# Turning half of the router's input inside the output projection of a two-layer transformer kernel

## The chip, the cores and the metric

The kernel runs on one core of one Trainium2 chip. The metric is device time in microseconds (us) of one execution; lower is better. The kernel before was timed in three runs: 1039.24, 1039.88 and 1039.9 us, median 1039.88 us.

## The reference, cut to what matters

All arithmetic is float32 on 256 tokens of width 1024. A first block (dilated attention, latent attention, a dense feed-forward) is followed by a second block of two layers. Each layer of the second block ends in the same four steps, and these are what the change touches:

```
h = h + mix @ w_out                                   # output projection, 1024 x 1024
xn = rms_norm(h, ln_ffn[i])
g_prob = softmax(xn @ w_group + b_group)              # 4 groups
e_logits = xn @ w_expert + b_expert                   # 32 experts, the best 2 of the best group
h = h + sum over the chosen experts (silu(xn @ w_gate) * (xn @ w_up)) @ w_down
gate = sigmoid(rms_norm(h, ln_ple[i]) @ ple_w_gate[i])
h = h + gate * (p[i] @ ple_w_proj[i])                 # p: 256 embedding columns per token
```

The router's product `xn @ [w_group, w_expert]` is a sum over the 1024 columns of `h`. It can be summed in any order of the columns, as long as the gains `ln_ffn` and the rows of the router's weights stand in the same order.

## The kernel before, in words

**Layout.** `h` holds 128 tokens per partition row set, two token tiles (t = 0, 1) of 1024 columns. TensorE needs the columns on the partitions, so activations are turned first: a transpose of 128 tokens by 128 columns into PSUM, then an eviction to SBUF that multiplies by the gain of the norm that follows. `turn` (line 491) plans these in jobs of two 128-column blocks; a job writes PSUM bank 4 + m % 4, with m its running number, and is evicted by ScalarE or VectorE in turn (or by both where a high and a low part are made). `pe_turn` (806) turns a job for both tiles; `pe_turn_tiles` (787) turns all jobs for tile 0 when tile 0 is ready, then for tile 1; `take_turn` (816) is the eviction. Without `whole`, block k of a turn takes every eighth column, k, k+8, k+16 and so on, so that a block needs all of a row; with `whole=True` block k is the 128 neighbouring columns from 128 k.

**The output projection.** `linear` (442) cuts the 1024 output columns into two halves of 512. A half is four chunks of two 128-row blocks of weights; `pe_linear` (898) runs the halves in order, and in each chunk 12 matmuls of 512 columns (2 tiles, 2 blocks, 3 products of high and low parts). For each chunk ScalarE makes the high part of the weights and VectorE the low part (`split`, 954), through four pairs of buffers, so the parts of chunk n wait until TensorE is done with chunk n - 4. `take_linear` (977) is the order on VectorE: the four splits of the second half's weights first, and behind them the two sums `h = h + PSUM` of the first half (993). Both layers (jobs `l_nsa_o` and `l_moba_o`) follow this order. Behind the first half's sums VectorE makes the low parts of the first two experts' weights (1701), then sums the second half, tile 0 and tile 1. ScalarE makes those experts' high parts (1694) and then loads the table for square roots.

**The router.** `moe_and_ple` (630) plans it. On TensorE, `pe_moe_and_ple` (2025) turns the embedding rows (`t_embed`, one job, 4 transposes), then `t_moe`, four jobs of `h` by tiles, 16 transposes; `pe_route` (1562) multiplies each turned block by 36 router columns, `pe_turn_logits` (1571) turns the logits back, and then come the embedding product (`pe_embed`, 1591), the places and the gather of the sorted tokens. On ScalarE, `act_moe_and_ple` (2055) squares tile 0 for the norm (745), evicts `t_embed`, squares tile 1, evicts two of the four jobs of `t_moe` (877) and takes the root (749). On VectorE, `dve_moe_and_ple` (2082) evicts the other two jobs (882), refines the root in six short instructions (763 to 768), and copies the second half of the logit rows (1586).

**The loads.** SyncE issues the large loads in one order: the chunks of weights up to the output projection's, then the embedding's weights (`sp_embed`, 2124) once the attention has been mixed, then the experts' (`sp_experts`, 1384). The small operands, the router's weights and all gains among them, are issued at the start by GpSimd (2168), and everyone waits for all of them together at `wait_small` (718).

Of the kernel before, what the change touches and what calls it, by code (L numbers as in the profile page):

```python
# [17 lines left out]
D_MODEL, KB = 1024, 8  # L18
# [118 lines left out]
def build_program(nc, a, out):  # L137
# [90 lines left out]
    gains = {}  # L228
    for name in ("norm_mix_g", "norm_ffn_g", "ln_mix0", "ln_ffn0", "ln_ple0", "kv_norm", "ln_mix1", "ln_ffn1",
                 "ln_ple1"):  # L230
        gains[name] = sb(f"gain_{name}", [P, KB])
# [398 lines left out]
    def moe_and_ple(layer):  # L630
        n_moe[layer] = norm([(h, rows, D_MODEL)])
        t_embed[layer] = turn(embed[:, layer], 2, [(embed_turned, None)])
        t_moe[layer] = turn(h, KB, [(turned_x, gains[f"ln_ffn{layer}"])])
        expert_units()
        n_ple[layer] = norm([(h, rows, D_MODEL)])
        t_ple[layer] = turn(h, KB, [(x_high, gains[f"ln_ple{layer}"], x_low)])
        l_gate[layer] = linear(a["ple_w_gate_2"][layer], KB, D_MODEL, x_parts, ple_gate, "gate", n_ple[layer],
                               halved_end=layer == 1)
# [69 lines left out]
    for i in range(2):  # L708
        load_small(route_w[:, i, :, 0:4], a["moe_w_group_2"][i].rearrange("(p k) n -> p k n", k=KB))
        load_small(route_w[:, i, :, 4:36], a["moe_w_expert_2"][i].rearrange("(p k) n -> p k n", k=KB))  # L710
        load_small(route_b[:, i, 0:4], a["moe_b_group_2"][i].partition_broadcast(P))
        load_small(route_b[:, i, 4:36], a["moe_b_expert_2"][i].partition_broadcast(P))
        load_small(embed[:, i], a["p_2"][i, 0].rearrange("(t p) n -> p t n", p=P))
# [183 lines left out]

    def pe_linear(pe, jobs, turned_by=(), ahead=None):

        for group in zip(jobs[0::2], jobs[1::2]):  # L900
            for c, number in enumerate(group[0]["splits"]):
                if ahead is not None and group[0] is jobs[0] and c in ahead:
                    ahead[c]()
# [657 lines left out]

    def pe_route(pe, layer):
        for j in t_moe[layer]:
            wait_turned(pe, [j])
            for i in range(2):
                k = j["j"] + i
                mm = nc.tensor.matmul(bank[64 * i:64 * i + 36, 0, 0:TOKENS], route_w[:, layer, k, :], turned_x[:, k, :],
                                      start=k < 2, stop=k >= KB - 2)
# [22 lines left out]
    def pe_embed(pe, layer, t, half, blocks_here=range(2)):  # L1591

        if t == half == 0 and 0 in blocks_here:
            wait_turned(pe, t_embed[layer])
            pe.wait_ge(embed_landed, 16 * (layer + 1))
            wait_turned(pe, t_moe[layer])
# [361 lines left out]
    def dve_route(dve, layer):  # L1958
# [64 lines left out]
        dve_sort(dve, layer)  # L2023

    def pe_moe_and_ple(pe, layer):
        pe_turn(pe, t_embed[layer])
        pe_turn_tiles(pe, t_moe[layer], [took_at(j) for j in (l_nsa_o if layer == 0 else l_moba_o)[-2:]])
        pe_route(pe, layer)
# [26 lines left out]
    def act_moe_and_ple(act, layer):  # L2055
        added = (l_nsa_o if layer == 0 else l_moba_o)[-2:]
        act_square_tile(act, n_moe[layer], 0, took_at(added[0]))
        take_turn(act, t_embed[layer], "act")
        act_square_tile(act, n_moe[layer], 1, took_at(added[1]))
        take_turn(act, t_moe[layer], "act")  # L2060
        act.wait_ge(squares_summed, n_moe[layer]["sums"] + TILES)
# [20 lines left out]
    def dve_moe_and_ple(dve, layer):  # L2082
        take_turn(dve, t_embed[layer], "dve")
        take_turn(dve, t_moe[layer], "dve")
        dve_norm(dve, n_moe[layer])
# [31 lines left out]
    def sp_chunk(sp, n):  # L2117
# [4 lines left out]
        sp.dma_start(c["view"], c["src"]).then_inc(c["landed"][0], 16)  # L2122

    def sp_embed(sp, layer):
        sp.wait_ge(mixed, (att_m["first"] if layer == 0 else n_heads[0]) // 4)
# [3 lines left out]
    def _(sp):  # L2129
# [5 lines left out]
        for n in range(unit_at[0], unit_at[1]):  # L2135
            sp_chunk(sp, n)
        sp_embed(sp, 0)
        sp_experts(sp, 0)
        for n in range(unit_at[1], unit_at[2]):
            sp_chunk(sp, n)  # L2140
        sp_embed(sp, 1)
        sp_experts(sp, 1)
# [98 lines left out]
    def _(pe):  # L2241
# [135 lines left out]
        pe.wait_ge(c_taken, 4)  # L2377
        pe_linear(pe, l_nsa_o, t_mix2, ahead={1: turn_last(t_mix2, c_taken, 4)})
        pe_moe_and_ple(pe, 0)
# [27 lines left out]
        pe.wait_ge(biased, n_heads[0])  # L2407
        pe_linear(pe, l_moba_o, t_mix3, ahead={1: turn_last(t_mix3, mixed, n_heads[0] // 4)})
        pe_moe_and_ple(pe, 1)

    @block.scalar
    def _(act):
# [137 lines left out]
        act_cast_expert(act, 0, 1)  # L2550
        nc.scalar.preload_act_table(ACT.Sqrt)
        act_moe_and_ple(act, 0)
        take_turn(act, t_moba, "act")
# [38 lines left out]
        act_cast_expert(act, 1, 1)  # L2592
        nc.scalar.preload_act_table(ACT.Sqrt)
        act_moe_and_ple(act, 1)

    @block.vector
    def _(dve):
# [179 lines left out]
        dve_split_expert(dve, 0, 0)  # L2777
        dve_split_expert(dve, 0, 1)
        take_linear(dve, l_nsa_o[2:], "dve")
        wait_took(dve, l_nsa_o)  # L2780
# [44 lines left out]
        dve_split_expert(dve, 1, 0)  # L2825
        dve_split_expert(dve, 1, 1)
        take_linear(dve, l_moba_o[2:], "dve")
        wait_took(dve, l_moba_o)
# [33 lines left out]
```

## Time and profile before

| what | value |
|---|---|
| median of three runs | 1039.88 us (1039.24 to 1039.9) |
| the profiled execution's own time | 1036.4 us |
| its span, which the profile shows | 1034.6 us |
| TensorE matmul | busy 1009.3 us of the span |
| VectorE, ScalarE, GpSimd | busy 765.3, 699.1 and 110.2 us |
| output projections of the two layers | about 467 to 490 us and 782 to 805 us |
| experts of the two layers | about 517 to 680 us and 832 to 995 us |

Times inside the span count from its start. A line of the timeline gives the start, the length, the engine, the source line, the operation with what it writes and reads, and how many instructions it merges; a part in brackets is idle time before it and who ended it. PE is TensorE's matmuls (transposes among them), PEld its weight loads, DVE is VectorE, ACT ScalarE, POOL GpSimd, and SPq SyncE's queue of loads. Matmul ends are modelled, so the starts of the next ones tell TensorE's pace. The chain of waits is followed back from the last instruction to whatever released each step; it is what sets the end.

### The profile page before, as it was taken

How to read it: one execution, taken by the hardware profiler on the slowest of the kernel's cores; microseconds unless marked ns; L12 is line 12 of the kernel's file. 1: busy time of each engine (PE TensorE's matmuls, PEld its weight loads, DVE VectorE, ACT ScalarE, POOL GpSimd, SP SyncE). 2: the span in 40 equal slices, each digit the busy share in tenths (PEclk: the TensorE clock that was granted, in tenths of full speed). 3: DMA queues.
4: the chain of work that ended last, by engine and by line, in shares of the span. 5: the costliest groups of instructions: out<-in, count | busy, mean ns of one | idle time of the engine just before them, and what ended most of it. 6: DMA issues, size and time to landing. Idle time of an engine off the chain costs nothing.

```text
span 1034.6 us, 17514 instructions
## 1 busy us (share of the span) xinstructions
PE 1009.3 (98%) x6141; PEld 843.8 (82%) x6141; DVE 765.3 (74%) x1350; ACT 699.1 (68%) x1207; POOL 110.2 (11%) x194
## 2 busy tenths in 40 slices
PE   7999999999999999999999999999999999999998
PEld 6887889999998877888688787877888688787877
DVE  5597666566666657877778888887887778888876
ACT  6675644444445536756698899857686598898955
POOL 9019000000000100300520000000000430000000
PEclk9999999999999999999999999999999999999999
DMA  9971047656554655004459999854514449999942
GB/s 294 298 258 64 1 155 231 183 182 195 178 174 163 190 182 205 2 17 148 182 213 326 337 338 335 303 183 145 164 58 163 183 161 322 331 345 334 330 141 72
DMA packets 107820, 209.25 MB, mean 202 GB/s; under 512 B 7864, under 2 KB 54432, under 8 KB 107488
## 3 DMA queue, kind: packets, MB, share of 16 engines
q1 hardware_dynamic: 105248, 204.04, 57.6%
q0 software_dynamic: 2064, 3.25, 1.2%
q8 instruction: 43, 0.70, 0.3%
q10 hardware_dynamic: 432, 0.99, 0.3%
q14 instruction: 33, 0.27, 0.1%
HBM read 207.19 MB, written 1.06 MB: 201 GB/s over the span
## 4 chain that ended last, share of the span: by engine, by line
PE 84%; DVE 7%; ACT 4%; DMA 2%; issue 2%; SPq 0%; ACTq 0%; DVEq 0%
PE bank L1774 18%; PE bank L919 12%; PE bank L1796 11%; PE bank L934 9%; PE bank L1420 9%; PE bank L1430 8%; PE bank L1068 4%; PE bank L1057 2%; PE bank L1032 2%; PE bank L812 2%; DVE weight_parts L969 1%; PE bank L1818 1%; PE bank L1598 1%; DMA expert_w<-in_moe_w_up 1%; PE bank L1637 1%
## 5 line engine op out<-in xcount | busy, mean ns | idle before, releaser
L1774 PE MATMUL bank<-expert_high,block_high 128*128 128x256 f32 x560 | 183.1, 328 | 1.5 <-ACT block_high L1717 1.3
L1701 DVE TENSOR_TENSOR expert_low<-expert_w,expert_high 128x1024 fp32r<-128x1024 f32 x140 | 164.9, 1221 | 8.0 <-ACT expert_high L1694 7.7
L1774 PE MATMUL bank<-expert_low,block_high 128*128 128x256 f32 x560 | 157.4, 282 | 0.0
L1694 ACT CAST expert_high<-expert_w 128x1024 fp32r<-128x1024 f32 x140 | 140.1, 1051 | 22.2 <-DMA expert_w<-in_moe_w_up 21.3
L1774 PE MATMUL bank<-expert_high,block_low 128*128 128x256 f32 x544 | 153.6, 282 | 0.0
L969 DVE TENSOR_TENSOR weight_parts<-ring,weight_parts 128x1024 fp32r<-128x1024 f32 (+3 forms) x116 | 122.3, 1081 | 40.2 <-ACT weight_parts L966 39.7
L966 ACT CAST weight_parts<-ring 128x1024 fp32r<-128x1024 f32 (+3 forms) x116 | 104.2, 928 | 63.8 <-PE bank L919 26.3
L919 PE MATMUL bank<-weight_parts,x_high 128*128 128x512 f32 (+3 forms) x544 | 145.7, 355 | 0.4 <-DVE weight_parts L969 0.4
L1796 PE MATMUL bank<-expert_w,junk 128*128 128x512 f32 x280 | 131.4, 593 | 0.0
L1774 PEld LDWEIGHTS bank<-expert_high,block_high 128*128 128x128 f32 x560 | 106.8, 191 | 18.5 <-issue 14.3
L1774 PEld LDWEIGHTS bank<-expert_low,block_high 128*128 128x128 f32 x560 | 106.8, 191 | 15.0 <-issue 15.0
L919 PEld LDWEIGHTS bank<-weight_parts,x_high 128*128 128x128 f32 x544 | 95.8, 188 | 15.2 <-DVE weight_parts L969 0.8
L1774 PEld LDWEIGHTS bank<-expert_high,block_low 128*128 128x128 f32 x544 | 103.7, 191 | 0.0
L1420 PE MATMUL bank<-x_high,parts 128*128 128x256 f32 x512 | 97.5, 283 | 0.4 <-ACT x_high L877 0.3
L919 PE MATMUL bank<-weight_parts,x_low 128*128 128x512 f32 (+3 forms) x272 | 96.1, 353 | 0.0
L1430 PE MATMUL bank<-parts,hid_parts 128*128 128x512 f32 x384 | 92.9, 391 | 0.0
L1852 DVE SCALAR_TENSOR_TENSOR arena<-bank,home_w,arena 128x1024 f32 x64 | 82.2, 1284 | 8.5 <-issue 4.8
L1420 PEld LDWEIGHTS bank<-x_high,parts 128*128 128x128 f32 x512 | 82.1, 191 | 2.2 <-issue 0.7
L1430 PEld LDWEIGHTS bank<-parts,hid_parts 128*128 128x128 f32 x384 | 70.1, 188 | 13.3
L1796 PEld LDWEIGHTS bank<-expert_w,junk 128*128 128x128 f32 x280 | 47.7, 190 | 34.4 <-issue 34.3
L1717 ACT CAST block_high<-sorted_high 128x1024 fp32r (+1 forms) x70 | 73.3, 1049 | 0.4 <-ACT sorted_high L1673 0.4
L1420 PE MATMUL bank<-x_low,parts 128*128 128x256 f32 x256 | 72.4, 283 | 0.0
(389 smaller groups left out, 1824.6 us busy)
## 6 DMA issues: line engine op xcount, KB each, us to landing
expert_w<-in_moe_w_gate SPq DMA_DIRECT2D x70, 512.0 KB, 5.7
expert_w<-in_moe_w_up SPq DMA_DIRECT2D x70, 512.0 KB, 7.3
expert_w<-in_moe_w_down SPq DMA_DIRECT2D x70, 512.0 KB, 5.6
ring<-in_w_ff SPq DMA_DIRECT2D x64, 512.0 KB, 3.9
ring<-in_w_in SPq DMA_DIRECT2D x16, 512.0 KB, 8.5
ring<-in_a_w_in SPq DMA_DIRECT2D x16, 512.0 KB, 6.5
ring<-in_ple_w_gate SPq DMA_DIRECT2D x12, 512.0 KB, 5.3
ring<-in_w_o SPq DMA_DIRECT2D x8, 512.0 KB, 5.4
```

The lines of the kernel that those rows point to most:

```text
L919: mm = nc.tensor.matmul(bank[:, j["m"] % 4, 0:n], j["operand"][x][:, 2 * c + kk, at[0]:at[1]], weight_parts[:, number % PAIRS, w, kk * n:( ...
L934: return nc.tensor.matmul(bank[:, j["m"] % 4, 0:n], j["operand"][x][:, 2 * c + kk, j["t"] * P:(j["t"] + 1) * P], weight_parts[:, number % ...
L966: nc.scalar.copy(high, raw_weights).then_inc(weights_high, 1)
L969: nc.vector.tensor_tensor(low, raw_weights, high, ALU.subtract).then_inc(weights_split, 1)
L1420: mm = nc.tensor.matmul(bank[:, b, 0:256], parts[:, u % 2, w, k * P:(k + 1) * P], x[:, k, :], start=k == 0 and n == 0, stop=k == KB - 1 an ...
L1430: mm = nc.tensor.matmul(bank[:, 2 * t + half, :], hid_parts[:, u % 2, x, t * P:(t + 1) * P], parts[:, u % 2, w, 2048 + half * 512:2048 + ( ...
L1694: nc.scalar.copy(half_of(expert_high[:, b % 2, :], j), half_of(expert_w[:, b % DEPTH, 0:2048], j)).then_inc(ex_cast, 1)
L1701: nc.vector.tensor_tensor(half_of(expert_low[:, b % DEPTH, 0:2048], j), half_of(expert_w[:, b % DEPTH, 0:2048], j), half_of(expert_high[:, ...
L1717: nc.scalar.copy(block_high[:, b % 2], sorted_high[:, :, ds(at, P)]).then_inc(ex_copied, 1)
L1774: mm = nc.tensor.matmul(to, x[:, b % 2, k, :], w[:, k], start=k == 0 and n == 0, stop=k == KB - 1 and n == 2)
L1796: mm = nc.tensor.matmul(bank[:, 2 * (b % 2) + half, :], hidTs[:, b % 2, :], expert_w[:, b % DEPTH, 2048 + half * 512:2048 + (half + 1) * 5 ...
L1852: v.scalar_tensor_tensor(out=here, in0=bank[:, 2 * (b % 2):2 * (b % 2) + 2, :].rearrange("p b n -> p (b n)"), scalar=share_of, in1=here, o ...
```

## The change

The router's turn of `h` is made in blocks of neighbouring columns (`whole=True`), so that its first two jobs need only the first half of the output projection. These two jobs and the embedding's one are turned inside the second half of the projection, ahead of its second chunk, and evicted by ScalarE and VectorE ahead of the sums of the second half. The router's weights and a second copy of the gains come in the order of neighbouring columns; they are now loaded by SyncE, three loads per layer ahead of the embedding's weights, and counted on the same semaphore `embed_landed`. The gains in the old order stay, since the sorted tokens still use them.

```diff
     for name in ("norm_mix_g", "norm_ffn_g", "ln_mix0", "ln_ffn0", "ln_ple0", "kv_norm", "ln_mix1", "ln_ffn1",
-                 "ln_ple1"):
+                 "ln_ple1", "route0", "route1"):
...
-        t_moe[layer] = turn(h, KB, [(turned_x, gains[f"ln_ffn{layer}"])])
+        t_moe[layer] = turn(h, KB, [(turned_x, gains[f"route{layer}"])], whole=True)
...
-        load_small(route_w[:, i, :, 0:4], a["moe_w_group_2"][i].rearrange("(p k) n -> p k n", k=KB))
-        load_small(route_w[:, i, :, 4:36], a["moe_w_expert_2"][i].rearrange("(p k) n -> p k n", k=KB))
...
-    def pe_linear(pe, jobs, turned_by=(), ahead=None):
+    def pe_linear(pe, jobs, turned_by=(), ahead=None, inside_last=None):
 
         for group in zip(jobs[0::2], jobs[1::2]):
             for c, number in enumerate(group[0]["splits"]):
+                if inside_last is not None and group[1] is jobs[-1] and c == 1:
+                    inside_last()
...
     def pe_route(pe, layer):
+        pe.wait_ge(embed_landed, 64 * (layer + 1))
...
-            pe.wait_ge(embed_landed, 16 * (layer + 1))
+            pe.wait_ge(embed_landed, 64 * (layer + 1))
...
+    def pe_turn_first_half(pe, layer):
+        pe_turn(pe, t_embed[layer])
+        pe.wait_ge(*took_at((l_nsa_o if layer == 0 else l_moba_o)[1]))
+        pe_turn(pe, t_moe[layer][:2])
+
     def pe_moe_and_ple(pe, layer):
-        pe_turn(pe, t_embed[layer])
-        pe_turn_tiles(pe, t_moe[layer], [took_at(j) for j in (l_nsa_o if layer == 0 else l_moba_o)[-2:]])
+        pe_turn_tiles(pe, t_moe[layer][2:], [took_at(j) for j in (l_nsa_o if layer == 0 else l_moba_o)[-2:]])
...
         act_square_tile(act, n_moe[layer], 0, took_at(added[0]))
-        take_turn(act, t_embed[layer], "act")
         act_square_tile(act, n_moe[layer], 1, took_at(added[1]))
-        take_turn(act, t_moe[layer], "act")
+        take_turn(act, t_moe[layer][2:], "act")
...
     def dve_moe_and_ple(dve, layer):
-        take_turn(dve, t_embed[layer], "dve")
-        take_turn(dve, t_moe[layer], "dve")
+        take_turn(dve, t_moe[layer][2:], "dve")
...
+    def sp_route(sp, layer):
+        for dest, src in ((gains[f"route{layer}"][:, :], a["ln_ffn_2"][layer].rearrange("(k p) -> p k", k=KB)),
+                          (route_w[:, layer, :, 0:4], a["moe_w_group_2"][layer].rearrange("(k p) n -> p k n", k=KB)),
+                          (route_w[:, layer, :, 4:36], a["moe_w_expert_2"][layer].rearrange("(k p) n -> p k n", k=KB))):
+            sp.dma_start(dest, src, allow_slow_non_contiguous=True).then_inc(embed_landed, 16)
...
+        sp_route(sp, 0)
         sp_embed(sp, 0)
         sp_experts(sp, 0)
...
-        pe_linear(pe, l_nsa_o, t_mix2, ahead={1: turn_last(t_mix2, c_taken, 4)})
+        pe_linear(pe, l_nsa_o, t_mix2, ahead={1: turn_last(t_mix2, c_taken, 4)},
+                  inside_last=lambda: pe_turn_first_half(pe, 0))
...
         nc.scalar.preload_act_table(ACT.Sqrt)
+        take_turn(act, t_embed[0], "act")
+        act.wait_ge(embed_landed, 64 * 0 + 64)
+        take_turn(act, t_moe[0][:2], "act")
         act_moe_and_ple(act, 0)
...
         dve_split_expert(dve, 0, 0)
         dve_split_expert(dve, 0, 1)
+        take_turn(dve, t_embed[0], "dve")
+        dve.wait_ge(embed_landed, 64 * 0 + 64)
+        take_turn(dve, t_moe[0][:2], "dve")
         take_linear(dve, l_nsa_o[2:], "dve")
```

The second layer has the same edits with its own jobs. The jobs alternate between the two evicting engines, so `t_embed` and the second and fourth job of `t_moe` fall to ScalarE, the first and third to VectorE, in both layers.

## Rows read from the trace of the kernel before

**Rows 1.** The page: TensorE's busy line, and the chain by engine.

```profile
PE 1009.3 (98%) x6141; PEld 843.8 (82%) x6141; DVE 765.3 (74%) x1350; ACT 699.1 (68%) x1207; POOL 110.2 (11%) x194
...
PE 84%; DVE 7%; ACT 4%; DMA 2%; issue 2%; SPq 0%; ACTq 0%; DVEq 0%
```

**Rows 2.** Chain of waits, first layer's projection: start us, us, what.

```profile
470.26 0.87 PE bank L812 x8
471.14 8.18 PE bank L934 x36
479.31 9.54 PE bank L919 x42
```

**Rows 3.** Timeline, TensorE, first matmuls of the second half's second chunk, both layers.

```profile
481.87 0.62 PE L919 MATMUL bank<-weight_parts,x_high 128*128 128x512 f32 x2
...
796.70 0.61 PE L919 MATMUL bank<-weight_parts,x_high 128*128 128x512 f32 x2
```

**Rows 4.** Timeline, VectorE, around the first half's sums, first and second layer.

```profile
480.49 1.23 DVE L969 TENSOR_TENSOR weight_parts<-ring,weight_parts 128x1024 fp32r<-128x1024 f32 x1 [1.49 <-ACT weight_parts L966]
481.63 1.28 DVE L993 TENSOR_TENSOR h<-h,bank 128x512 f32<-128x512 f32 x2
482.82 4.63 DVE L1701 TENSOR_TENSOR expert_low<-expert_w,expert_high 128x1024 fp32r<-128x1024 f32 x4
...
796.46 1.28 DVE L993 TENSOR_TENSOR h<-h,bank 128x512 f32<-128x512 f32 x2
```

**Rows 5.** Chain of waits elsewhere: eight transposes of `h` right after a wait.

```profile
331.26 1.16 PE bank L795 x8
```

**Rows 6.** Chain of waits, first layer, from the projection's end to the logits.

```profile
488.87 0.70 DVE h L993
...
489.59 1.15 ACT rows L745 x2
490.74 0.55 ACT junk L867
491.29 1.05 ACT rows L745 x2
492.34 1.55 ACT second L877 x4
493.89 0.19 ACT stat L749
...
495.34 0.44 DVE work L1586
...
495.82 1.08 PE bank L1575 x8
```

**Rows 7.** Timeline, the same stretch, engines beside that chain.

```profile
485.81 1.28 ACT L2551 ACT_TABLE_LOAD   x1
...
490.04 0.63 PE L812 MATMUL bank<-table,embed 128*128 128x128 f32 x4
490.24 0.69 DVE L993 TENSOR_TENSOR h<-h,bank 128x512 f32<-128x512 f32 x1 [0.68 <-PE bank L919]
490.51 2.22 PE L795 MATMUL bank<-table,h 128*128 128x128 f32 x16
...
491.19 1.06 ACT L745 ACTIVATE rows<-h 128x1024 f32<-128x1024 f32 x1
```

**Rows 8.** Chain of waits, first turn of the shared keys: every eighth column.

```profile
723.51 1.75 PE bank L812 x16
```

**Rows 9.** Waits of SyncE's queue: us in total, times, longest.

```profile
SPq L2126 <- DVE part L1197: 59.6, 1, 59.6
...
SPq L2126 <- DVE mix L1197: 32.2, 1, 32.2
```

**Rows 10.** DMA issues: the embedding's weights, KB each, median us from issue to landing.

```profile
arena<-in_ple_w_proj SPq DMA_DIRECT2D x2, 1024.0 KB, 4.8
```

**Rows 11.** Line 1346 (feed-forward weights, 512 KB each, 512-byte runs): issue to landing.

```profile
DMA to landing us min/median/max: 3.7/3.9/5.7
```

More of the change, by code:

```diff
@@ L2140, in _ @@
             sp_chunk(sp, n)
+        sp_route(sp, 1)
         sp_embed(sp, 1)
@@ L2407, in _ @@
         pe.wait_ge(biased, n_heads[0])
-        pe_linear(pe, l_moba_o, t_mix3, ahead={1: turn_last(t_mix3, mixed, n_heads[0] // 4)})
+        pe_linear(pe, l_moba_o, t_mix3, ahead={1: turn_last(t_mix3, mixed, n_heads[0] // 4)},
+                  inside_last=lambda: pe_turn_first_half(pe, 1))
         pe_moe_and_ple(pe, 1)
@@ L2593, in _ @@
         nc.scalar.preload_act_table(ACT.Sqrt)
+        take_turn(act, t_embed[1], "act")
+        act.wait_ge(embed_landed, 64 * 1 + 64)
+        take_turn(act, t_moe[1][:2], "act")
         act_moe_and_ple(act, 1)
@@ L2826, in _ @@
         dve_split_expert(dve, 1, 1)
+        take_turn(dve, t_embed[1], "dve")
+        dve.wait_ge(embed_landed, 64 * 1 + 64)
+        take_turn(dve, t_moe[1][:2], "dve")
         take_linear(dve, l_moba_o[2:], "dve")
```

## The prediction

> **What bounds the kernel now.** The page comes first: TensorE is busy 1009.3 of 1034.6 us and holds 84% of the chain that ends last [rows 1]. What is put onto TensorE's path therefore costs its full length, unless TensorE waits at that place anyway; what leaves another engine pays only where that engine holds the chain. So the second question is which engine holds the chain at the place that instructions leave, and at the place that they go to. The chain of waits, cut to that stretch, answers both.
>
> In the projection it is TensorE alone. From 471.14 us on there are 36 matmuls in 8.18 us and then 42 in 9.54 us, 0.227 us each without a gap [rows 2]. At its end the chain leaves TensorE: VectorE's sum of tile 0, ScalarE's square of tile 0, its copy of the turned embedding, its square of tile 1, its four evictions, its root, then VectorE's refinement and copy, and TensorE turns the logits back at 495.82 us [rows 6]. No transpose and no router product stands in that chain: TensorE's transposes of 490.04 and 490.51 us run beside ScalarE [rows 7]. The change thus takes work off ScalarE, where ScalarE sets the pace, and moves transposes from a place where they are hidden to one where TensorE sets the pace. The second layer repeats the pattern (its projection ends near 804 us), so each term counts twice.
>
> **What the projection pays.** Ahead of the second half's second chunk TensorE gets 12 transposes, 4 of the embedding and 8 of `h`, and a wait between them.
> - The place in time is 481.87 us, the first matmul of that chunk [rows 3].
> - The embedding's 4 need nothing late. Eight transposes inside the first half of the same projection, read from neighbouring columns, took 0.87 us, 0.109 each [rows 2]; sixteen that read every eighth column took 1.75 us, 0.109 as well [rows 8], so I count one price for both orders. Four cost 0.44 us, until 482.31.
> - Then TensorE waits for the first half's sums. VectorE's queue has the last low part of weights ahead of them (480.49 us, 1.23 us long, itself late because ScalarE's high part had to wait for TensorE), and the two sums run from 481.63 for 1.28 us, until 482.91 [rows 4]. Nothing that the change does comes ahead of them on VectorE. TensorE so stands still from 482.31 to about 482.93 (0.02 us from the end of a sum to whoever waits, as from 489.57 to 489.59 in rows 6).
> - Eight transposes that begin right behind a wait took 1.16 us until the next matmul, not 0.87 [rows 5]. So the chunk starts at 484.09 and not at 481.87: **2.22 us** later. With 1.16 replaced by 0.87 it is 1.93; with no wait at all it is 12 x 0.109 = 1.31.
> - The second layer is the same to a hundredth: chunk at 796.70 [rows 3], sums until 796.46 + 1.28 = 797.74 [rows 4].
>
> Behind that nothing gives the time back: the remaining three chunks have their weights (the last low part is done at 481.72 [rows 4]) and go on at 0.227 us a matmul.
>
> **What is hidden.** VectorE's added evictions (two instructions) fall between the experts' low parts, done at 482.82 + 4.63 = 487.45, and the next sum at 488.87, which the change moves to about 491.1 [rows 4, 6]. ScalarE's added copy and two evictions follow its table load, done at 487.09 [rows 7]: 0.55 + 0.78 us [rows 6], finished near 488.5. Both covers are over 2 us; without them the sums and squares would start later by what overlaps.
>
> **What the end of the projection gets back.** The sum of tile 1 ends at 490.24 + 0.69 = 490.93; the square of tile 1 began at 491.19, since the embedding's copy was ahead of it, and can now begin at 490.95: 0.24 us [rows 7]. Two of the four evictions go, 1.55 / 2 = 0.78 us [rows 6]. The root, VectorE's refinement, its copy and the logits follow unchanged, so the gain is **1.02 us**. If the square should start no earlier, it is 0.78. VectorE, with one job left, is done before the root, and so are the router's products: their first two jobs are ready early and ScalarE's last eviction ends near 492.9, over 1 us before the refinement does. What is late next is ScalarE still: squares, two evictions, root. After the logits everything shifts as a whole.
>
> **The loads.** GpSimd issues four loads fewer at the start, when TensorE has other work; I count nothing. SyncE issues three more per layer, ahead of the embedding's weights, and there its queue waits 59.6 and 32.2 us for the attention to be mixed [rows 9]. They are in small runs: 1024 runs of 4, of 16 and of 128 bytes. The trace has no such load. The nearest row, 512 KB in 1024 runs of 512 bytes, lands in 3.9 us, at most 5.7 [rows 11], so three take 4 us if they overlap and 17 us one after another at the worst; either is covered. I count nothing, and keep the late case as a rival. The Trainium skill's page "DMA: Bandwidth & Descriptors", "Rules for kernel authors", speaks against this edit: a last dimension with a stride becomes one descriptor per element, to be avoided by rearranging. By it the loads would be slow, and the time that of rival 3; by the row they stay hidden.
>
> The embedding's weights are issued ahead of the projection's start (about 467 and 782 us) and take 4.8 us [rows 10]; the first wait for `embed_landed`, ScalarE's behind its table load at 487.09 [rows 7], comes 20 us behind that start. These waits cost nothing unless the loads are late, and then the squares and the last sums queue behind them.
>
> **The sum.** 2 x (2.22 - 1.02) = **+2.4 us**. Against the profiled execution's own 1036.4 us that is 1038.8; the median of the runs is 3.5 us above that execution, and on it the sum gives **1042.3 us**. The bounds: 2 x (1.93 - 1.02) = +1.8 and 2 x (2.22 - 0.78) = +2.9, so 1041.7 to 1042.8 for this case. About 0.2% (2.1 us) is what a measurement of this kernel can tell from no change.
>
> **The rivals.**
> 1. **No stall at the turn (not slower).** If the first half's sums were done before TensorE has turned the embedding, by 482.31, only the 12 transposes cost, 1.31 us: 2 x (1.31 - 1.02) = +0.6, 1040.5 us. It decides if the sums come 0.6 us earlier than in the trace. For it: their matmuls end near 479.3. Against it: the low part of 480.49 stands ahead of them in both layers.
> 2. **The projection absorbs the turns (faster).** If TensorE's steps had slack there, so that three later chunks made up for the insertion, only the gain would be left: 2 x -1.02 = -2.0, 1037.8 us. For it: TensorE's ends are modelled, and its weight parts are ready ahead. Against it: the eight transposes inside the first half were followed by the same 0.227 us a matmul [rows 2].
> 3. **Late small loads (much slower).** To be late in the second layer, the three loads would need 32.2 + 20 - 4.8 = 47 us, four times 3 x 3.9; at five times, 58 us, the second layer would be some 11 us late: about 1054 us. Only the smallness of the runs speaks for it.
>
> That the change does not do what it says is excluded by its diff: both jobs need the first half only.
>
> **How the numbers follow.** The forecast gets 0.57: its rows are from the very place. Rival 1 gets 0.19, rival 2 0.11, rival 3 0.04, and 0.09 is for what I have not seen (0.03 faster, 0.03 same, 0.03 slower). Of the forecast's 0.57 some 0.42 lies above 1042.0, the rest within 0.2%. That makes faster 0.14, same 0.37, slower 0.49. The range reaches from rival 1 to the forecast's upper bound, each widened by the 0.7 us that the runs before differ by: 1039.8 to 1043.5, without rivals 2 and 3. The forecast's own range is 1041.7 to 1042.8.
>
> **What the next profile should show.** In the chain of waits inside the projection: 4 transposes, then VectorE's sum of `h` as a link, then 8 transposes, and the last matmul 2.2 us later after the first half's start. At the end: sum, square, square, two evictions, root, with the embedding's copy gone, and 5.9 us instead of 6.95 from the first sum to the turned logits. I am wrong on the stall if TensorE's idle time ahead of those 8 transposes is under 0.2 us; wrong on the gain if the stretch from sum to logits is shortened by under 0.7 or over 1.4 us; and wrong on the loads if anyone waits for `route_w` or the embedding's weights.

## The result and the profile after

| what | before | after |
|---|---|---|
| median beside each other | 1039.39 us (6 runs, 1035.96 to 1039.9) | 1047.93 us (6 runs, 1045.68 to 1050.16) |
| ratio, 95% interval | 1 | 1.0089 (1.0069 to 1.0108) |
| profiled execution, its span | 1036.4, 1034.6 us | 1047.52, 1045.7 us |

The kernel became 0.9% slower. The forecast was 1042.3 us, with a range up to 1043.5: the sign was right, the size was not, and the range did not hold it.

The mean granted clock is recorded for each run and differs between runs of one kernel, so each kernel below also gets an estimate of its time at full clock, which is time multiplied by that mean, averaged over the runs. That this holds can be seen on the kernel before: of its 96 runs beside all the experiments, 49 at 0.999 or 1.000 average 1037.1 us and 47 at 0.996 or 0.997 average 1040.7; the difference of 3.6 us is what 0.0034 of the clock is of the span (3.5 us). In the three groups that these runs came in, the estimate for the kernel before is 1037.0, 1036.9 and 1036.6 us.

The chain of waits of the kernel after, first layer, from the projection to the logits (start us, us, what); it answers to [rows 2, 4, 6]:

```profile
473.05 8.19 PE bank L934 x36
...
483.62 1.21 DVE h L993 x2
...
484.87 1.09 PE bank L810 x8
485.96 8.21 PE bank L919 x36
...
494.20 0.70 DVE h L993
...
494.92 1.15 ACT rows L743 x2
496.07 0.73 ACT second L875 x2
496.80 0.19 ACT stat L747
...
497.21 1.28 DVE stat L762
```

The insertion is there as predicted, with VectorE's sum of `h` as a link ahead of the eight transposes, and ScalarE's part is one square and two evictions shorter. New is the line of 497.21: the second step of the root's refinement takes 1.28 us. The timeline of the same stretch shows what lies beside it, and what comes behind (start us, length, engine, line, and in brackets the idle time before). Its first line shows TensorE's wait for the first half's sums inside the projection, called the stop below: 0.64 us by the weight loads.

```profile
484.87 0.85 PEld L810 LDWEIGHTS bank<-table,h 128*128 128x128 f32 x8 [0.64 <-DVE h L993]
...
492.83 0.69 DVE L993 TENSOR_TENSOR h<-h,bank 128x512 f32<-128x512 f32 x1 [2.69 <-PE bank L919]
...
494.94 3.51 POOL L1536 MEMSET arena<- 128x4096 f32 x1 [52.77 <-DVE h L993]
...
495.49 0.88 DVE L880 TENSOR_SCALAR second<-bank,gain_route 128x256 f32<-128x256 f32 x2 [0.61 <-PE bank L793]
...
497.01 0.17 DVE L761 RECIPROCAL stat<-stat 128x2 f32<-128x2 f32 x1 [0.64 <-ACT stat L747]
497.21 1.27 DVE L762 TENSOR_SCALAR stat<-stat 128x2 f32<-128x2 f32 x1
...
499.78 1.08 PE L1576 MATMUL bank<-table,work 36*128 36x36 f32 x8 [2.30 <-DVE work L1587]
500.79 7.11 PE L1599 MATMUL bank<-arena,junk 128*128 128x512 f32 x12
```

GpSimd clears the experts' accumulators from the last sum on, 494.94 to 498.45, and VectorE's step ends at 498.48. The same lines of the kernel before:

```profile
490.98 3.51 POOL L1536 MEMSET arena<- 128x4096 f32 x1 [50.75 <-DVE h L993]
...
494.31 0.21 DVE L764 TENSOR_SCALAR stat<-stat 128x2 f32<-128x2 f32 x1
...
495.82 1.08 PE L1575 MATMUL bank<-table,work 36*128 36x36 f32 x8 [0.80 <-DVE work L1586]
496.83 5.42 PE L1598 MATMUL bank<-arena,junk 128*128 128x512 f32 x12
```

There the clearing ended at 494.49, just as the step of 494.31 needed it: the kernel before missed the collision by the microsecond that the change takes off ScalarE. So the stretch from the first sum to the turned logits is 499.78 - 492.83 = 6.95 us after, and 495.82 - 488.87 = 6.95 us before. TensorE is done with the router's products 1.5 us earlier after that sum (2.30 - 0.80), so it stands still for 2.30 us and not 0.80, and then the embedding product takes 7.11 us and not 5.42. Its granted clock (busy times, then the clock, the DMA share and GB/s) of the two layers:

```profile
500.00:502.00 2.00, 2.00 (x11) 1.42 (x11) 0.90 (x5) 1.49 (x2) 0.00 (x0) 1.00 1.04 422
502.00:504.00 2.00, 2.00 (x3) 0.67 (x2) 1.73 (x9) 0.58 (x1) 0.00 (x0) 0.51 1.01 414
...
818.00:822.00 4.00, 3.16 (x10) 2.06 (x11) 2.17 (x11) 2.44 (x3) 0.00 (x0) 0.68 1.03 423
822.00:826.00 4.00, 4.00 (x6) 1.69 (x5) 3.52 (x17) 0.58 (x1) 0.00 (x0) 0.50 1.03 413
```

0.50 is the lower level, 1.2 GHz. In the second layer the step was held too (816.27, 1.28 us); the product took 8.40 us, and the logits' turn ahead of it 1.36 us and not 1.08. The loads stayed hidden: SyncE's queue needed 0.47 and 0.62 us to issue the gains, up to 5.49 and 3.31 us for the two parts of the router's weights, and still waits 50.5 and 27.2 us for the attention behind them [rows 9]; nobody waits for them.

```profile
L2131 SPq DMA_DIRECT2D gain_route<-in_ln_ffn x2: 469/546/623, 404.8 to 756.1; - x2
L2131 SPq DMA_DIRECT2D route_w<-in_moe_w_group x2: 903/3195/5487, 405.5 to 756.6; - x2
...
SPq L2135 <- DVE part L1197: 50.5, 1, 50.5
...
SPq L2135 <- DVE mix L1197: 27.2, 1, 27.2
```

A tail, here and below, is the stretch from the projection's end to the end of the embedding product. So the 11.1 us between the two spans are: 1.9 us that are there before the projection (these 36 matmuls start at 473.05 and 471.14 [rows 2]; number 4 below, the same code up to there, starts them at 471.14 too, so they are not the change's), 2 x 2.05 us of insertion (first sum at 492.83 against 488.87, less that 1.9), nothing from the first sum to the logits, and 1.7 and 3.3 us of halved clock, some 11 in all. Over all runs: mean time 1048.0 at a mean clock of 0.9942, against 1038.9 at 0.9980; at full clock 1041.8 (standard error 0.6) against 1036.8 (0.1). That is 5.0 us of work and waits, and 4.0 us of clock. The 5.0 is, within its error, the predicted 2.4 and the 2.1 of gain that did not arrive.

### The profile page after: what moved, and what is told of

Same layout as the page of the kernel before. It is cut to its first block, busy times and chain, and to the rows that moved or that the text cites. A ratio compares the mean times of both kernels' runs of the same rounds, so it can differ in the third digit from the quotient of the medians.

```text
span 1045.7 us, 17522 instructions
## 1 busy us (share of the span) xinstructions
PE 1016.8 (97%) x6141; PEld 846.6 (81%) x6141; DVE 767.9 (73%) x1350; ACT 698.8 (67%) x1207; POOL 107.5 (10%) x190
## 4 chain that ended last, share of the span: by engine, by line
PE 84%; DVE 7%; ACT 4%; DMA 2%; issue 2%; SPq 0%; ACTq 0%; DVEq 0%
PE bank L1775 17%; PE bank L919 11%; PE bank L1797 11%; PE bank L934 9%; PE bank L1420 9%; PE bank L1430 8%; PE bank L1068 4%; PE bank L1057 2%; PE bank L1032 2%; PE bank L810 2%; PE bank L1599 1%; DVE weight_parts L969 1%; PE bank L1819 1%; DMA expert_w<-in_moe_w_up 1%; PE bank L1638 1%
```

## The experiments

The theory behind the experiments: the insertion costs what was predicted; ScalarE's gain is real, but it moves VectorE's refinement under GpSimd's clearing, which holds it; and TensorE's longer idle time ahead of the logits brings its clock down. The rivals: the turns, the stop in the projection, or the loads and the new order disturb the clock; or something other than the clearing holds VectorE.

All runs together. "Full clock" is the mean of time x granted clock with its standard error; the last column counts profiled tails (two per profile, both of one execution) in which the clock fell. The ratio is to runs of the kernel before in the same group. "Exchange" means that VectorE copies its logit rows ahead of the root's refinement and not behind it.

| kernel | median us | ratio to before (95%) | mean clock | full clock, us | idle ahead of the logits, us | tails with a fall |
|---|---|---|---|---|---|---|
| before (96 runs) | 1039.0 | 1 | 0.9980 | 1036.8 (0.1) | 0.80 | 0 of 2 |
| after | 1047.93 | 1.0089 (1.0069 to 1.0108) | 0.9942 | 1041.8 (0.6) | 2.30 | 2 of 2 |
| 1 clearing early | 1041.34 | 1.0020 (1.0003 to 1.0038) | 0.9974 | 1039.0 (0.4) | 1.20 | 1 of 2 |
| 2 gap filled | 1044.81 | 1.0052 (1.0029 to 1.0075) | 0.9980 | 1042.8 (0.4) | 0 | 0 of 2 |
| 3 before, clearing late | 1044.10 | 1.0053 (1.0034 to 1.0072) | 0.9955 | 1040.1 (0.3) | 2.27 | 1 of 2 |
| 4 third chunk | 1042.56 | 1.0063 (1.0037 to 1.0089) | 0.9947 | 1039.4 (0.4) | 2.30 | 2 of 2 |
| 5 early, third chunk | 1040.30 | 1.0023 (1.0000 to 1.0047) | 0.9968 | 1038.3 (0.2) | 1.20 | 2 of 2 |
| 6 the same, exchange | 1038.55 | 0.9991 (0.9974 to 1.0008) | 0.9978 | 1036.5 (0.3) | 0.53 | 0 of 2 |
| 7 before, exchange | 1037.75 | 0.9987 (0.9971 to 1.0003) | 0.9982 | 1036.5 (0.4) | 0.53 | 0 of 2 |
| 8 order and loads | 1037.96 | 0.9995 (0.9977 to 1.0013) | 0.9989 | 1037.3 (0.2) | 0.74 | 0 of 2 |
| 9 early, gap filled | 1040.93 | 1.0025 (1.0007 to 1.0042) | 0.9984 | 1039.5 (0.3) | 0 | 0 of 2 |
| 10 before, attention | 1039.84 | 1.0001 (0.9983 to 1.0020) | 0.9972 | 1036.3 (0.4) | 0.80 | 0 of 2 |
| 11 exchange, attention | 1037.82 | 0.9994 (0.9976 to 1.0011) | 0.9982 | 1036.2 (0.3) | 0.53 | 0 of 2 |
| 12 turns and all | 1037.82 | 0.9989 (0.9972 to 1.0005) | 0.9981 | 1036.3 (0.2) | 0.53 | 0 of 2 |

**1. The clearing behind the first half's sums.**

```diff
-        wait_took(pool, l_nsa_o if layer == 0 else l_moba_o)
+        pool.wait_ge(*took_at((l_nsa_o if layer == 0 else l_moba_o)[1]))
         nc.gpsimd.memset(acc, 0.0).then_inc(acc_zeroed, 1)
```

> The kernel after, with GpSimd's clearing of the experts' accumulators (3.51 us) started behind the first half's sums of the projection and not behind its last sum. Theory (the clearing holds VectorE's second refinement step for 1.06 us, the gap ahead of the logits' turn so grows to 2.30 us, and TensorE's clock falls behind that gap): that step takes 0.2 us again and not 1.27, the refinement 1.2 and not 2.26, the gap 1.2, and the stretch from the first sum to the turned logits 5.9 and not 6.95; if the shorter gap keeps the clock at 1.00, the twelve matmul passes of the embedding product take 5.4 us in both layers and not 7.0 and 8.4: some 6.8 us less than the kernel after, about 1041. Rival A (the clock falls because of the stop and the transposes inside the projection, or because TensorE does less in the whole tail, and not through the gap): the step is short, but the clock still falls, 2.1 us less, about 1046. Rival B (something else holds VectorE's step): nothing changes, about 1048.

Measured: 1041.34 us. The timeline of this kernel, GpSimd, VectorE and then TensorE in both layers:

```profile
486.49 3.53 POOL L1536 MEMSET arena<- 128x4096 f32 x1 [42.77 <-DVE h L993]
...
498.84 0.17 DVE L762 TENSOR_SCALAR stat<-stat 128x2 f32<-128x2 f32 x1
...
500.31 1.08 PE L1576 MATMUL bank<-table,work 36*128 36x36 f32 x8 [1.20 <-DVE work L1587]
501.32 5.42 PE L1599 MATMUL bank<-arena,junk 128*128 128x512 f32 x12
...
817.34 7.11 PE L1599 MATMUL bank<-arena,junk 128*128 128x512 f32 x12
```

The step takes 0.17 us, and from the first sum (494.45) to the logits (500.31) it is now 5.86 us, the prediction's 5.9. The clearing was what held the step, and rival B falls. At full clock the kernel is 2.2 us above the kernel before, where the prediction's sum was +2.4. The clock still fell in one tail of two (the gap was 1.20 us in both), so the hope that the shorter gap would keep it up held only in part.

**2. The gap filled, the clearing left where it was.**

```diff
     def pe_turn_logits(pe, layer):
+        for k in range(7):
+            nc.tensor.matmul(bank[0:36, 2, 0:TOKENS], route_w[:, layer, k, :], turned_x[:, k, :],
+                             start=True, stop=True)
         pe.wait_ge(logit_rows_kept, 2 * (layer + 1))
```

> The kernel after, with seven router products done a second time into a bank that nobody reads, behind the router's last product, so that TensorE works through most of the gap ahead of the logits' turn (14 matmul passes of 0.122 us, 1.7 us, in a gap of 2.30). Theory (the clock falls because TensorE stands still for 2.30 us there): granted clock 1.00 in both tails, embedding product 5.4 us in both layers and not 7.0 and 8.4, 4.7 us less than the kernel after, about 1043; VectorE's second refinement step still takes 1.27 us. Rival A (the stop or the transposes inside the projection, or the loads, bring the clock down): it falls all the same, about 1048.

Measured: 1044.81 us.

```profile
497.02 3.19 PE L1574 MATMUL bank<-second,route_w 128*36 128x256 f32 x14
500.14 1.08 PE L1579 MATMUL bank<-table,work 36*128 36x36 f32 x8
501.15 5.42 PE L1602 MATMUL bank<-arena,junk 128*128 128x512 f32 x12
...
819.09 5.42 PE L1602 MATMUL bank<-arena,junk 128*128 128x512 f32 x12
```

The filling took 3.19 us, not 1.7: each pass 0.228 us. All its products went to one half of a bank, where the router's own alternate between two halves (0.122). It overran the gap by some 0.7 us a layer, which is why the full-clock time is 1 us above the kernel after. With TensorE at work the clock stayed at 1.00 in both tails and the product took 5.42 us, with the stop and the turns inside the projection in place, and the mean clock over its six runs is 0.9980, the kernel before's. That speaks against rival A.

**3. The kernel before with the clearing 1.4 us later.**

```diff
         wait_took(pool, l_nsa_o if layer == 0 else l_moba_o)
+        pool.wait_ge(squares_summed, n_moe[layer]["sums"] + TILES)
         nc.gpsimd.memset(acc, 0.0).then_inc(acc_zeroed, 1)
```

> The kernel before, with one change: GpSimd's clearing of the accumulators waits for the square of the second token tile, so that it runs about 1.5 us later (some 492.5 to 496.0 and not 490.98 to 494.49) and lies over VectorE's refinement. Nothing is turned inside the projection. Theory: VectorE's second refinement step takes some 1.7 us and not 0.21, the gap ahead of the logits' turn grows from 0.80 to some 2.3 us, the granted clock falls there and the embedding product takes 7 to 8.4 us and not 5.4: 1.5 us and 1.7 to 3.0 us in each layer, 6 to 9 us slower than the kernel before. Rival A (the clock falls through the turns inside the projection): 2 x 1.5 us slower, clock 1.00. Rival B (the clearing does not hold VectorE): no change.

Measured: 1044.10 us, ratio 1.0053.

```profile
492.36 3.51 POOL L1537 MEMSET arena<- 128x4096 f32 x1 [52.22 <-ACT rows L745]
...
494.20 1.69 DVE L764 TENSOR_SCALAR stat<-stat 128x2 f32<-128x2 f32 x1
...
497.19 1.08 PE L1576 MATMUL bank<-table,work 36*128 36x36 f32 x8 [2.27 <-DVE work L1587]
498.20 5.42 PE L1599 MATMUL bank<-arena,junk 128*128 128x512 f32 x12
...
815.14 8.22 PE L1599 MATMUL bank<-arena,junk 128*128 128x512 f32 x12
```

Without any turn inside the projection the two missing terms appear: the step takes 1.69 us (495.89, when the clearing ends at 495.87), the gap is 2.27 us in both layers, and the clock falls behind it in one of them. At full clock it is 3.3 us above the kernel before, against 2 x 1.47 = 2.9 from the gaps. None of its ten runs has a mean clock above 0.997, where 49 of 96 of the kernel before have. Less than the 6 to 9 us of the theory, since the clock does not fall every time.

**4. The turns ahead of the third chunk.**

```diff
-                if inside_last is not None and group[1] is jobs[-1] and c == 1:
+                if inside_last is not None and group[1] is jobs[-1] and c == 2:
```

> The kernel after, with the turns ahead of the third chunk of the second half and not ahead of its second, when the first half's sums are long done. Prediction's step (12 transposes of 0.109 us, a wait for the sums, a slow start behind the wait): without the wait they cost 1.3 to 1.5 us and not 2.16, so 0.65 to 0.85 us less in each layer. Theory on the tail: nothing there changes, the gap stays 2.3 us and the clock falls as in the kernel after, so 1.3 to 1.7 us less in all, about 1046.4. Rival A (the stop inside the projection is what brings the clock down later): clock 1.00 in the tails, another 4.7 us less, about 1041.7.

Measured: 1042.56 us, and its nine runs lie at 1042 (five) or 1047 to 1049 (four, clock 0.992), so the median says little. The chain of waits:

```profile
471.14 8.18 PE bank L934 x36
479.32 5.45 PE bank L919 x24
484.76 1.35 PE bank L810 x12
...
491.61 0.70 DVE h L993
```

Twelve transposes take 1.35 us, with no stop, and the last sum at 491.61 against 490.24 [rows 7], both from a first half at 471.14: 1.37 us and not 2.05. The difference, 0.68 us, is the stop (0.64 us). The clock fell in both tails (7.11 us each), with no stop in the projection: the stop is not its cause.

**5 to 8. Parts together, and the order and loads alone.** Number 5 has the edits of 1 and 4. Number 6 has this one more, which number 7 puts into the kernel before:

```diff
-        dve_norm(dve, n_moe[layer])
         dve_keep_logit_rows(dve, layer)
+        dve_norm(dve, n_moe[layer])
```

Number 8 is the kernel after without anything inside the projection (the evictions on ScalarE and VectorE move back likewise):

```diff
-        pe_turn_tiles(pe, t_moe[layer][2:], [...])
+        pe_turn(pe, t_embed[layer])
+        pe_turn_tiles(pe, t_moe[layer], [...])
...
-                  inside_last=lambda: pe_turn_first_half(pe, 0))
```

Number 5, expected:

> The kernel after with both edits: the clearing of the accumulators behind the first half's sums, and the turns ahead of the third chunk. Theory (the change costs its insertion, less what ScalarE gives back; the clock falls where TensorE stands still for long or does little): the insertion costs some 1.4 us a layer and not 2.16, the refinement takes 1.2 us, so at full clock 2 x (1.4 - 1.03) = +0.8 us against the kernel before; the gap ahead of the logits' turn is 1.2 us and the clock falls behind it in half of the tails at the most. Together +0.5 to +2.5 us, 1039.5 to 1041. Rival (the turns inside the projection bring the clock down by themselves): falls in both tails, +5 us.

Number 6, expected:

> As the kernel before this in the list, and VectorE copies its half of the logit rows ahead of the root's refinement and not behind it. Theory (with ScalarE's evictions gone, VectorE's queue order holds the logits, since the router's products are done before the refinement): the logits are turned some 0.7 us earlier, the gap shrinks to 0.5 us, the route starts 0.55 to 0.7 us earlier. At full clock 2 x (1.4 - 1.03 - 0.6) = -0.5 us against the kernel before, and no fall of the clock in the tails: 1037 to 1039, level with or just below the kernel before. Rival (the route waits for the refinement, which now ends later): no gain from the exchange, +0.8 us and more, 1039.5 to 1041.

Number 7, expected:

> The kernel before with the same exchange on VectorE alone: logit rows copied ahead of the refinement. The router's products there end at 494.97 us and the refinement some 0.5 us later, so the logits are turned 0.35 us earlier and the route starts 0.2 to 0.35 us earlier: -0.4 to -0.7 us in all, within what can be told from no change. It tells whether a gain of the kernel with the exchange and the turns comes from the turns at all: if that kernel is not below this one, the turns are worth nothing.

Number 8, expected:

> The kernel after with nothing turned inside the projection: the turn by neighbouring columns, the router's weights in that order and SyncE's three loads per layer stay, and the embedding and all four jobs are turned at the end of the projection as in the kernel before. Theory (the new order and its loads cost nothing): the same as the kernel before within 0.2%, gap ahead of the logits' turn 0.8 us, refinement 1.2 us, clock 1.00 in both tails. Rival (the loads or the order of columns cost something, or disturb the clock): slower by 2 us or more, or falls in the tails.

Measured: 1040.30, 1038.55, 1037.75 and 1037.96 us. Number 5 at full clock is 1.5 us above the kernel before (0.8 expected), with falls in both profiled tails behind gaps of 1.20 us; four of its ten runs are at 1.000, so the rival, a fall in every tail, does not hold. Number 8 is not told apart from the kernel before: order and loads cost nothing that shows. For number 6 the timeline gives

```profile
499.75 0.43 DVE L1587 COPY work<-bank 36x256 f32<-36x256 f32 x1 [1.16 <-PE bank L1568]
...
500.23 1.08 PE L1576 MATMUL bank<-table,work 36*128 36x36 f32 x8 [0.53 <-DVE work L1587]
501.24 5.42 PE L1599 MATMUL bank<-arena,junk 128*128 128x512 f32 x12
```

The copy no longer waits for the refinement, the gap is 0.53 us, and the clock stays up in both tails. Number 6 is 9 us below the kernel after, and level with the kernel before (0.9974 to 1.0008). But number 7, with no turn moved at all, is level with it too (0.9971 to 1.0003), so nothing here shows a gain from the turns.

**9. The early clearing, and the rest of the gap filled,** with eight products that alternate between the halves of a bank:

```diff
+        for k in range(8):
+            nc.tensor.matmul(bank[64 * (k % 2):64 * (k % 2) + 36, 2, 0:TOKENS], route_w[:, layer, k, :],
+                             turned_x[:, k, :], start=True, stop=True)
```

> The kernel after with the clearing of the accumulators behind the first half's sums (the gap ahead of the logits' turn is then 1.20 us, and the clock fell behind it in one tail of two), and eight router products done a second time into a bank that nobody reads, some 1.0 us, in that gap. Theory (what is left of the falls in the tails comes from the gap): no fall in either tail, embedding product 5.4 us in both, 1.7 us less than with the gap where it fell; at full clock 2.1 us above the kernel before as without the filling, so 1039 to 1041. Rival (the turns inside the projection or the changed order of work cause the falls): one or two tails still fall, 1041 to 1043.

```profile
497.35 1.90 PE L1574 MATMUL bank<-second,route_w 128*36 128x256 f32 x16
499.18 1.08 PE L1579 MATMUL bank<-table,work 36*128 36x36 f32 x8
500.18 5.42 PE L1602 MATMUL bank<-arena,junk 128*128 128x512 f32 x12
```

Measured: 1040.93 us, no fall in a profiled tail, and six of ten runs at 0.999 or 1.000, as often as the kernel before; with the gap open (number 1) it was one of ten. The filling overran the gap again, by half a microsecond (499.18 - 495.56 = 3.62 us from the first product to the logits, against 3.15 in number 1), so its median shows no gain. Turns, stop and order are all in place, and only the idle time is gone, so the falls in the tails come from that gap. The filling also gives TensorE more to do; whether standing still or doing little brings the clock down, numbers 2 and 9 do not tell.

**10 to 12. Where the kernel before itself loses its clock.** Number 10 fills the 0.94 us of idle time ahead of the second block's attention; 11 is the same with the exchange of 7, 12 the same with all of 6.

```diff
         wait_turned(pe, t_nq + t_nk[:1])
+        for _ in range(3):
+            nc.tensor.matmul(bank[:, 4 + t_nk[0]["m"] % 4, 0:P], ident, ident, start=True, stop=True)
         wait_took(pe, l_g)
```

Number 10, expected:

> The kernel before, with three products of the identity with itself (6 matmul passes of 128 columns, some 0.7 us) into a free bank in the 0.94 us in which TensorE waits ahead of the second attention's first scores (409.7 to 410.6 us). The traces of three kernels show the clock fallen from about 414 to 423 us, behind this gap and in a stretch of narrow matmuls; about half of the runs of the kernel before have a mean granted clock of 0.996 and are some 4 us longer. Theory (this gap starts that fall): all runs at 0.999 or 1.000, median 1037, 1.9 us below the mean of the kernel before. Rival (the narrow matmuls behind the gap bring the clock down, with or without the gap): half of the runs still at 0.996, median as before.

Number 11, expected:

> The kernel before with the logit rows copied ahead of the refinement and the same three products ahead of the attention's scores. If these start the fall: 1036.5, 0.2% below the kernel before, nearly all runs at 0.999 or 1.000. If not: as with the exchange alone, about 1038.

Number 12, expected:

> The turns ahead of the third chunk, the clearing behind the first half's sums, the logit rows copied ahead of the refinement, and the three products ahead of the attention's scores. If the turns are worth nothing beside the exchange: level with the kernel before this in the list within 0.1%. If the turns gain something of their own once stop, clearing and clock are out of the way: below it by 0.5 us or more; if they still cost something, above it.

Measured: 1039.84, 1037.82 and 1037.82 us; seven of ten, six of twelve and six of twelve runs still at 0.996 or 0.997. The profiles of 6, 7, 10 and 12, executions of that kind, all have the fall at 416 to 424 us; those of executions at 1.000 (before, 2, 8, 9 and 11) have none. Number 10's timeline, and its granted clock:

```profile
411.76 0.83 PE L2359 MATMUL bank<-table 128*128 128x128 f32 x6
412.57 1.58 PE L1032 MATMUL bank<-ring 64*128 64x128 f32 x16
...
414.26 4.30 PE L1239 MATMUL bank<-kcT,ring 128*128 128x32 f32 x32
```

```profile
416.00:420.00 4.00, 4.00 (x28) 3.67 (x29) 2.50 (x7) 2.35 (x11) 2.56 (x3) 0.66 0.00 0
420.00:424.00 4.00, 4.00 (x19) 2.37 (x18) 2.39 (x13) 1.64 (x8) 0.64 (x2) 0.50 0.00 0
```

TensorE was busy throughout from 408 us to this fall, so the theory of these three runs is wrong: the fall comes without the gap. What is left is the stretch of narrow products behind it; that was not tried. Twelve against eleven is the fairest price of the turns: the same median, and 1036.3 against 1036.2 us at full clock. With stop, clearing and the falls in the tails out of the way the turns gain nothing that these runs can show (standard errors 0.2 and 0.3 us). No version is shown to beat the kernel before.

## Why the prediction was wrong

- **The insertion: right.** Predicted 2.22 us a layer, measured 2.05. The wait was there (0.64 us against 0.62), the eight transposes behind it took 1.09 and not 1.16, and rival 1 (no stall) falls. Number 4 shows the wait's share by taking it away.
- **Nothing given back in the projection: right.** 36 matmuls in 8.21 us after the turns, 0.228 each; rival 2 falls.
- **ScalarE's gain: right in itself.** The last sum to the root's end: 494.20 to 496.99 against 490.24 to 494.08 [rows 6, 7], 2.79 us and not 3.84, so 1.05 against the predicted 1.02.
- **The step that failed: "The root, VectorE's refinement, its copy and the logits follow unchanged", and with it "What is late next is ScalarE still".** The refinement did not follow unchanged. Its second step, moved a microsecond closer to the last sum, fell under GpSimd's clearing, which starts at that sum and takes 3.51 us whatever ScalarE does. Late next was GpSimd, and the gain of 2.1 us was gone; the prediction named the stretch of 6.95 us as the sign of that. Number 1 gives the 5.86 us back, number 3 makes the same loss in the kernel before. The rows that the prediction rests on are those of the chain's engines; the clearing stands in GpSimd's, and ended 0.2 us after the refinement's second step had begun.
- **The second failed step: "After the logits everything shifts as a whole".** It priced TensorE's instructions behind the gap at their old durations. The gap grew from 0.80 to 2.30 us, the clock fell in both tails, and over the runs the clock accounts for 4.0 us. None of the rivals had it; of the 0.09 for what was not seen, a third was for slower.
- **The loads: right.** The Trainium skill's page "DMA: Bandwidth & Descriptors", "Rules for kernel authors", has one descriptor per element where the last dimension has a stride. Of the three loads that is the gains' alone; the prediction held the rule against all three. The trace does not show that load slow to issue (0.62 and 0.47 us); the slow ones (up to 5.49 and 3.31 us) are the router's weights, whose last dimension has no stride. All stayed hidden, and number 8 shows no price.

The sum of the two terms, +2.4 us, is what number 1 measures at full clock (+2.2, standard error 0.4). With the 2.1 us of gain that did not arrive and the 4.0 us of clock it makes 8.5, where the means of the runs differ by 9.1. The two terms of the change were understood; what it set off on GpSimd and VectorE, and in TensorE's clock, was not.

That the fall of the clock in the tails goes with the gap is shown by the tails together: 0 of 18 fell where TensorE stood still for 0.80 us or less, 3 of 4 at 1.20, 5 of 6 at 2.27 or 2.30; and filling the gap, with all else in place, took the falls away (numbers 2 and 9). Why the same gap sometimes does and sometimes does not bring it down stays open.

## What to carry to other kernels

When a chain gets shorter, look at everything that runs beside its new place, on all engines: work started by the same event as the chain (here a clearing off the critical path) may stand in the way of the step that now comes earlier. Price the idle time that a change gives TensorE not only as idle time, but also by what the products behind it cost at half clock. And where runs of one kernel differ by a few microseconds, set their times beside their granted clocks before a difference of half a per cent is read.

## What the runs showed of the hardware

- GpSimd's clearing held VectorE's TENSOR_SCALAR from SBUF to SBUF, of two elements per partition, until its own end (0.17 us became 1.27 and 1.69), while RECIPROCAL of the same shape, at 497.01 in the midst of the clearing, took 0.17 us, and the two scalings out of PSUM at 495.49, in its midst too, took 0.88 us, as without it in number 1 (497.12, 0.88 us). The Trainium skill's page "SBUF — State Buffer", "Who interferes with whom", has this rule: a scaling or copy of VectorE that can use both its port pairs shares one of them with GpSimd, and who issues first holds it for the whole instruction. The times agree: in the kernel after the step ends 0.03 us behind the clearing, in number 3 it ends 0.02 us behind it. That the ports are the reason no run here shows.
- The clock fell to 1.2 GHz behind idle times of 1.20 to 2.30 us, in 8 of 10 profiled tails; and between 416 and 424 us also with TensorE at work on narrow products without a gap. The Trainium skill's page "TensorE: Matmul & The Clock Gate", Part 1, ties the two levels to how busy TensorE has been. The rows agree: the granted clock is 1.00 or 0.50 for whole stretches, filling the gap keeps it up (numbers 2 and 9), and number 10 shows a fall with no idle time ahead of it.
- Products of 36 output rows took 0.228 us a pass into one half of a bank, and 0.119 alternating between two halves (3.19 us for 14 and 1.90 us for 16).
